# An MoE decode step: expert chunks of 32 rows instead of 64, their results summed in PSUM instead of gathered from DRAM

## What is computed

```python
def moe_ffn(h, w_router, b_router, w_up, b_up, w_down, b_down):
    xt = h.reshape(-1, D)                                   # 288 x 1024
    logits = (xt @ w_router + b_router).astype(jnp.float32)
    top_v, top_i = lax.top_k(logits, TOP_K)                 # 4 of 32
    wts = jax.nn.softmax(top_v, axis=-1)
    gate_dense = jnp.sum(jax.nn.one_hot(top_i, N_EXPERTS) * wts[..., None], axis=1)
    out = jnp.zeros_like(xt)
    for e in range(N_EXPERTS):
        z = xt @ w_up[e] + b_up[e]                          # 1024 -> 2048
        gate = jnp.minimum(z[:, :D_EXPERT], SWIGLU_LIMIT)
        up = jnp.clip(z[:, D_EXPERT:], -SWIGLU_LIMIT, SWIGLU_LIMIT)
        act = (up + 1.0) * gate * jax.nn.sigmoid(SWIGLU_ALPHA * gate)
        out = out + gate_dense[:, e:e + 1] * (act @ w_down[e] + b_down[e])   # 1024 -> 1024
    return out.reshape(B, T, D)
...
        y = y + g2 * rms_norm(moe_ffn(h, *moe_w), norm_ffn_post[l])
```

## Time and profile before

| | |
|---|---|
| median of 3 runs | 1501.06 us (1496.23 to 1505.27) |
| profiled execution | 1502.18 us |
| its span, first to last instruction | 1500.3 us |
| mean granted TensorE clock | 0.981 |
| TensorE matmul busy | 1391.5 us, 93% |
| VectorE, ScalarE, GpSimd busy | 372.8, 298.0, 80.3 us |
| moved by DMA | 513.31 MB, 342 GB/s over the span |
| chain that ended last | PE 70%, DMA 23%, VectorE 3% |

### The profile page before, as it was taken

How to read it: one execution, slowest core, us unless ns; L and a number is a source line. 1 busy time by engine, 2 the same in 40 slices (tenths; PEclk the granted TensorE clock), 3 DMA queues, 4 the chain that set the end, 5 groups by cost and what they waited for, 6 DMA issues and landing times.

```text
span 1500.3 us, 20784 instructions
## 1 busy us (share of the span) xinstructions
PE 1391.5 (93%) x8590; PEld 616.0 (41%) x8590; DVE 372.8 (25%) x858; ACT 298.0 (20%) x572; POOL 80.3 (5%) x107
## 2 busy tenths in 40 slices
PE   5999998799989999999999999999999998999894
PEld 4554555466766433333333333333333322333231
DVE  5220012377643531111121111211111111111125
ACT  5100005566421221101111111110111110111001
POOL 2000004000000000000000000000000000000000
PEclk9899999999999999999999999999999999999997
DMA  9985755124297899799999999999999999999995
GB/s 282 335 303 204 266 201 178 49 73 154 65 274 269 350 420 427 319 395 427 426 427 426 426 427 426 428 426 426 429 425 428 425 428 425 428 427 426 427 405 182
DMA packets 94787, 513.31 MB, mean 342 GB/s; under 512 B 12033, under 2 KB 41113, under 8 KB 67634
## 3 DMA queue, kind: packets, MB, share of 16 engines
q1 hardware_dynamic: 87986, 490.04, 81.8%
q0 software_dynamic: 6720, 22.06, 4.2%
HBM read 501.19 MB, written 19.22 MB: 347 GB/s over the span
## 4 chain that ended last, share of the span: by engine, by line
PE 70%; DMA 23%; DVE 3%; ACT 2%; issue 1%; SPq 1%; POOL 1%; POOLq 0%; DVEq 0%; ACTq 0%
PE bank L1460 21%; DMA arena<-in_w_up 18%; PE bank L1487 13%; PE bank L1417 5%; PE bank L818 4%; PE bank L1227 4%; PE bank L1058 3%; PE bank L1059 3%; DMA arena<-slots 2%; PE bank L1324 2%; DMA arena<-in_cache_cmp,arena 2%; PE bank L1450 1%; PE bank L1470 1%; PE bank L831 1%; PE bank L1423 1%
## 5 line engine op out<-in xcount | busy, mean ns | idle before, releaser
L1460 PE MATMUL bank<-arena 128*64 128x512 f32 x2176 | 481.5, 596 | 33.4 <-DMA arena<-in_w_up 33.4
L1460 PEld LDWEIGHTS bank<-arena 128*64 128x64 f32 x2176 | 150.6, 137 | 361.1 <-issue 300.4
L1487 PE MATMUL bank<-arena 128*64 128x512 f32 x1088 | 241.2, 595 | 0.4 <-DMA arena<-in_w_down 0.4
L2443 DVE TENSOR_SCALAR arena<-bank,arena 128x1 uint32<-128x1 f32 x33 | 7.2, 219 | 565.0 <-DMA slots<-arena 564.9
L1487 PEld LDWEIGHTS bank<-arena 128*64 128x64 f32 x1088 | 74.7, 136 | 141.1 <-issue 135.7
L1849 ACT ACTIVATE arena<-arena 128x512 f32<-128x512 f32 x34 | 21.4, 630 | 515.7 <-DVE arena L2447 515.7
L1417 PE MATMUL bank<-arena 128*64 128x512 f32 (+1 forms) x420 | 103.0, 607 | 0.0
L2543 POOL DMA_DIRECT2D slots<-arena x33 | 18.1, 547 | 1100.7 <-ACT arena L1859 1100.7
L1227 PE MATMUL bank<-arena 128*128 128x288 f32 x256 | 69.8, 420 | 2.9 <-DMA arena<-in_w_in 1.7
L2447 DVE TENSOR_SCALAR arena<-bank 128x512 f32<-128x512 f32 x34 | 23.5, 692 | 189.5 <-PE bank L1460 189.5
L1859 ACT COPY arena<-bank 128x512 f32<-128x512 f32 x33 | 19.3, 585 | 214.9 <-PE bank L1487 214.9
(11 more groups left out here) (455 smaller groups left out, 1242.0 us busy)
## 6 DMA issues: line engine op xcount, KB each, us to landing
arena<-in_w_up SPq DMA_DIRECT2D x128, 2048.0 KB, 33.3
arena<-in_w_down SPq DMA_DIRECT2D x64, 2048.0 KB, 33.0
arena<-in_w_ada SPq DMA_DIRECT2D x12, 2048.0 KB, 11.6
arena<-in_w_in SPq DMA_DIRECT2D x6, 2048.0 KB, 12.2
arena<-in_w_in SPq DMA_DIRECT2D x16, 512.0 KB, 4.3
arena<-in_state_win SPq DMA_DIRECT2D x4, 1024.0 KB, 10.6
arena<-in_w_out SPq DMA_DIRECT2D x1, 4096.0 KB, 17.4
arena<-slots SPq DMA_DIRECT2D x2, 2048.0 KB, 25.1
```

What stands on the lines that cost most here:

```text
L1460: last = mm(banks[part][SLOT * s:SLOT * s + SLOT, :], xcT[:, q], ring[n % R_][:, at:at + 512], start=False, stop=q == 7)
L1487: last = mm(banks[4][SLOT * s:SLOT * s + SLOT, :], lhs, ring[n % R_][:, at:at + 512], start=f == 0, stop=f == 7)
```

## The change

SLOT becomes 32. Of a chunk, 32 rows take a quarter of the output partitions, and four instructions with 32 columns of the array each stand side by side, each for another quarter of the weights' columns. `slots`, the indirect writes, `slot_rows` and the gather at the end are gone. Instead PSUM banks 3 to 7 hold the sums of all tokens through all experts: banks 4 to 7 the 256 prompt tokens, bank 3 the 32 sample tokens. After each chunk TensorE adds the chunk *before* to them: `owT` (the weights of that chunk's 32 rows by token, transposed) times `yc`. These products (L1462, L1468 of the new file) stand in the chunk behind the transposes of the activations and ahead of three transposes that make the next `owT` (L1456, L1457) and of the down products. The order of the transposes is turned: `chunk_T` first, then the activations'. The down biases are added once, ahead of expert 1. The rows of a `w_down` piece are laid out so that each partition gets two runs of 8 KB instead of one of 16 KB.

```diff
-SLOT = 64
+SLOT = 32
...
+            def up_products(c, e):
+                for q in range(8):
+                    n = 6 * e + q // 2
+                    if q % 2 == 0:
+                        pe.wait_ge(S(f"ld_piece{n % R_}"), 16 * (n // R_) + 16)
+                    for j in range(4):
+                        last = mm(banks[0][32 * j:32 * j + SLOT].rearrange("p (h c) -> p h c", h=2), xcT[:, q % 2, q // 2],
+                                  up_cols[n % R_][:, q % 2, j], start=q == 0, stop=q == 7)
+                    if q == 0:
+                        for r in range(4):
+                            mm(banks[0][32 * r:32 * r + SLOT, :], ident[32 * r:32 * r + E, 32 * r + e:32 * r + e + 1].broadcast_to([E, SLOT]),
+                               bias[32 * r:32 * r + E, :], start=False, stop=False)
+                    if q % 2:
+                        last.then_inc(S("up_used"), 1)
...
+            def add_prompt(i, shares, rows, r, start, stop):
+                for q in range(4):
+                    last = mm(banks[4 + q][:, 256 * i:256 * i + 256], shares[32 * q:32 * q + r, P * i:P * i + P],
+                              rows[32 * q:32 * q + r, 0:256], start=start, stop=stop)
+                return last
...
             for e in range(E):
                 before = pe.value_load(tab[0:1, E + e:E + e + 1], min_val=0, max_val=CMAX)
                 upto = pe.value_load(tab[0:1, e:e + 1], min_val=1, max_val=CMAX)
+                if e == 1:
+                    pe.wait_ge(S("owT"), before + 1)
+                    down_biases()
                 with pe.Fori(before, upto) as c:
                     pe.wait_ge(S("xcT"), c + 1)
-                    if e > 0:
-                        slot_rows(e)
...
+                    pe.wait_ge(S("owT"), c + 1)
+                    up_products(c, e)
                     pe.wait_ge(S("oneslot"), c + 2)
+                    pe.wait_ge(S("yc"), c + 1)
                     dispatch()
-                    pe.wait_ge(S("act"), c + 1)
-                    for k in range(4):
-                        last = nc.tensor.transpose(banks[(3, 6)[k // 2]][:, P * (k % 2):P * (k % 2) + P], up_fours[:, k], ident)
...
                     pe.wait_ge(S("xr"), c + 2)
                     chunk_T()
-                    pe.wait_ge(S("yc"), c)
...
+                    pe.wait_ge(S("act"), c + 1)
+                    for v in range(2):
+                        last = nc.tensor.transpose(banks[1][:, P * v:P * v + P], act_pairs[:, v], ident)
+                    last.then_inc(S("aT_ps"), 1)
+                    for i in range(2):
+                        add_prompt(i, owT, yc, SLOT, False, False)
+                    add_sample(owT, yc, SLOT, False, False)
+                    pe.wait_ge(S("ow"), c + 1)
+                    weights_T()
+                    down_products(c, e)
...
+                if n == PIECES - 1:
+                    sp.wait_ge(S("up_used"), until * 4 + 3)
+                    sp.dma_start(gate_p, modd[0:1, 3 * D:4 * D].broadcast_to([P, D])).then_inc(S("ld_last"), 16)
...
+                if q < 4:
+                    sp.wait_ge(S("up_used"), until * 4 + (q + 1))
+                else:
+                    sp.wait_ge(S("down_used"), until * 2 + (q - 3))
                 load_piece(n)
...
-            with pool.Fori(0, last_chunk) as c:
-
-                pool.wait_ge(S("yc"), c + 1)
-
-                pool.dma_start(slots[bass.ds(NRES + c, 1), 0:1], eps_t[0:1]).then_inc(S("st_yc"), 16)
-                pool.indirect_dma_start(out=results, out_offset=bass.IndirectOffsetOnAxis(ap=rowu[:, 0:1], axis=0), in_=yc, in_offset=None,
-                                        bounds_check=2 * NRES - 1, oob_is_err=False).then_inc(S("st_yc"), 16)
```

More of the change, by code:

```diff
@@ new lines, in down_products @@
+            def down_products(c, e):
+                pe.wait_ge(S("aT"), c + 1)
+                for m in range(2):
+                    n = 6 * e + 4 + m
+                    pe.wait_ge(S(f"ld_piece{n % R_}"), 16 * (n // R_) + 16)
+                    for v in range(2):
+                        for h in range(2):
+                            for j in range(4):
+                                last = mm(banks[1][32 * j:32 * j + SLOT, 256:512], aT[:, v, 2 * m + h], down_cols[n % R_][:, h, v, j],
+                                          start=m + v + h == 0, stop=m + v + h == 3)
+                    last.then_inc(S("down_used"), 1)
@@ new lines, in add_sample, with down_biases @@
+            def add_sample(shares, rows, r, start, stop):
+                for q in range(4):
+                    last = mm(banks[3][32 * q:32 * q + NS, 0:256], shares[32 * q:32 * q + r, TP:TP + NS],
+                              rows[32 * q:32 * q + r, 0:256], start=start, stop=stop)
+                return last
+            def down_biases():
+                after(pe, "dense4")
+                for i in range(3):
+                    last = nc.tensor.transpose(banks[0][:, P * i:P * i + ROWS[i]], dense4[0:ROWS[i], i].rearrange("p q e -> p (q e)"),
+                                               ident[0:ROWS[i], 0:ROWS[i]])
+                last.then_inc(S("wT_ps"), 1)
+                pe.wait_ge(S("ld_bdown"), 64)
+                after(pe, "wT")
+                for i in range(2):
+                    add_prompt(i, wT, bdown, E, False, False)
+                add_sample(wT, bdown, E, False, False)
@@ L1499, in _ @@
-            summed_in = ((0, 1), (2, 3), (6, 7))
-            def biases(i):
-                for v in range(2):
-                    q = 32 * (2 * (i % 2) + v)
-                    mm(banks[summed_in[i][v]][0:ROWS[i], :], wT[q:q + E, P * i:P * i + ROWS[i]], bdown[q:q + E], start=True, stop=False)
-            def chunk_part(i):
-                r = ROWS[i]
-                for v in range(2):
-                    last = mm(banks[summed_in[i][v]][0:r, :], owT[SLOT * v:SLOT * v + SLOT, P * i:P * i + r], yc[SLOT * v:SLOT * v + SLOT],
-                              start=False, stop=i < 2)
-                return last
@@ L1513, in _ @@
-            after(pe, "wT")
-            pe.wait_ge(S("ld_bdown"), 64)
-            for i in range(3):
-                biases(i)
-            for i in range(2):
-                chunk_part(i).then_inc(S(f"sum{i}"), 1)
-            chunk_part(2)
-            pe.wait_ge(S("ld_gath2"), 64)
-            for v in range(2):
-                last = mm(banks[6 + v][0:NS, :], wdiag, gath_s[:, 512 * v:512 * v + 512], start=False, stop=True)
-            last.then_inc(S("comb_ps"), 1)
+                    pe.wait_ge(S("act"), c + 1)
@@ L1526, in _ @@
+            pe.wait_ge(S("owT"), upto + 1)
+            for i in range(2):
+                add_prompt(i, owT, yc, SLOT, False, i == 1)
+            add_sample(owT, yc, SLOT, False, True).then_inc(S("sums"), 1)
+            after(pe, "sample_ss")
+            for j in range(4):
+                last = mm(banks[2][32 * j:32 * j + NS, 0:1], C("stack32"), ss[:, 3:4], start=True, stop=True)
+            last.then_inc(S("sample_parts"), 1)
         @block.scalar
@@ new lines, in _ @@
+            with act.Fori(0, first) as c:
+                chunk_step(c)
+            after(act, "wT_ps")
+            nc.scalar.copy(wT, banks[0][:, 0:TP + NS]).then_inc(S("wT"), 1)
+            with act.Fori(first, total) as c:
+                chunk_step(c)
+            act.wait_ge(S("sums"), 1)
+            for half in range(2):
+                if half:
+                    act.wait_ge(S("half_gated"), 1)
+                for i in range(2):
+                    last = fn(squares[2 * half + i], prompt_sum(i, half), ACT.Square,
+                              accum_out=sq2[:, i, half:half + 1])
+                last.then_inc(S("half_squared"), 1)
@@ L1874, in _ @@
-            last.then_inc(S("sq2"), 1)
-            root(2, 8)
+            after(act, "sample_parts")
+            fn(rt_[:, 2:3], banks[2][:, 0:1], ACT.Sqrt, bias=eps_t, scale=1.0 / D).then_inc(S("rms"), 1)
         @block.vector
@@ L2471, in _ @@
[L2471 to L2480 removed]
+                dve.wait_ge(S("aT_ps"), c + 1)
```

357 lines of the change are left out of this document (140 added, 217 removed).

## The result

The changed kernel takes **1529.64 us** (median of 4 runs, 1526.59 to 1532.99), the kernel before on the same chip 1500.3 us (4 runs, 1496.23 to 1505.27). The ratio is 1.0195, with a 95% interval of 1.0154 to 1.0235. The forecast was 1527, in a range of 1492 to 1550. The profiled execution has a span of 1525.6 us, against 1500.3 before.

The account below looks back on a forecast made before the run. PE and DMA were both taken as full, to be priced per expert. 1500.3 - 11.4 - 11.0 + 54.6 + 1.5 + 1.5 + 4 - 13.4 = 1526.1 us span; +1.9 around it, median 1.1 lower: 1527, range 1492 to 1550.

Parts of the forecast that it names:

- T: PE's time for one chunk of 32 rows: 16.5 us, with bounds of 14.6 and 17.5.
- Stalls of 54.6: DMA waits for PE at experts with several chunks: 26.4 us in runs of two, 4.2 at expert 3, 24.0 at expert 13.
- The old stall, -11.4: DMA time lost at two-chunk expert 3 in the kernel before, taken off the sum: 11.4 us.
- Written results, -11.0: Result rows no longer written to DRAM (4.7 MB) free 11.0 us of DMA time.
- Gates ahead of the last piece, +1.5: The last gates (0.65 MB) are loaded ahead of the last weight piece: 1.5 us more.
- Rows of 8 KB, +1.5: Down pieces come in rows of 8 KB instead of 16 KB: between 0 and 3 us more, 1.5 taken.
- Clock, +4: PE's clock drops where it waits for pieces, on entering runs of two-chunk experts: 4 us more, bounds 0 and 7.
- Tail, -13.4: After the last piece, without the gather: 20.3 us at half clock against 33.7 before, 13.4 less.
- the first: Rival: DMA-bound all the way; with T at 14.8 or less two chunks fit into 29.7 us: 1485 us, chance 0.12.
- The second: Rival: terms cancel, T about 15.7 by cheaper changes of shape and no clock loss: 1503 us, chance 0.16.
- the fourth: Rival: waiting for activations replaces waiting for rows, 0.3 us more per chunk: 1533 us, counted in the forecast's chance of 0.64.
- The third: Rival: four side by side don't keep pace, or clock drops reach chunks; T 18 to 19.6, about 1605 us, chance 0.08.

Follow-up runs that it names:

- the chunks of 64 rows: Changed kernel with chunks of 64 rows again, 34 of them, keeping the new sums in PSUM: 1545.38 us, ratio 1.0292 to the kernel before.
- the stores' experiment: Kernel with one chunk of 32 per expert, plus 32 stores of 128 KB of results to unread DRAM: 1474.41 us, 8.9 more than without the stores.
- the kernel with 14.0: Changed kernel without the sums of all chunks' results but the last, and without the up products' bias: 1485.47 us, ratio 0.9869 to the kernel before.
- the last kernel: Changed kernel, same result: sums before the wait, sample rows last in dispatch, up bias and one register load per expert, last gates later: 1491.74 us, ratio 0.9931.

## Why the prediction was right, point by point

The time, the sign and the mechanism came out as forecast: 1529.6 for 1527, by DMA that waits for PE in runs of experts with two chunks. Inside the sum several terms were off and made each other good, which is luck.

- **T = 16.5**: 16.59 within an expert. The single terms are all within 0.2 of their rows: bias 1.0 for 1.05, dispatch with the wait 2.24 for 2.2, sums 1.08 and 0.56 for 1.0 and 0.55, down products 3.47 for 3.55. What was missing is the 0.4 between experts.
- **Stalls of 54.6**: 67 against a clean piece (expert 3: 5.5, experts 4 to 6: 13.2, expert 13: 26.7, experts 14 to 18: 21.9). For an expert of two chunks I had 33.0 - 29.7 = 3.3; it is 33.8 - 29.4 = 4.4. Of the 1.1, 0.3 is the price of a piece (4.95 for 4.90), 0.2 the chunks, 0.4 the change of expert. Experts 8, 9, 12 and those after 18 lost nothing, as said, but for a longer piece now and then.
- **The old stall, -11.4**: 12.8 in the same reckoning. That expert 3 shows what any expert with two chunks does was a wrong reading of the old trace: expert 13 lost 0.4 there (see the chunks of 64 rows above). **Written results, -11.0**: about -10, by the stores' experiment.
- **Gates ahead of the last piece, +1.5**: the last piece came 7.2 us after the one before it, 5.9 in the kernel before, so +1.3. **Rows of 8 KB, +1.5**: 0; the down pieces land every 4.9 us like the others.
- **Clock, +4**: next to nothing before the last piece in the profiled execution, and that was chance. In the first experts PE waits almost 3 us for each piece, and of two pieces with the same wait one is used at full clock (1.93; granted clock 1.00 from 592 to 596 us) and one at half (3.55; 0.53 from 597.3 to 600.9):

```profile
592.46 1.93 PE L1433 MATMUL psum<-arena 128*32 128x512 f32 x16 [2.97 <-DMA arena<-in_w_up]
597.35 3.55 PE L1433 MATMUL psum<-arena 128*32 128x512 f32 x16 [2.97 <-DMA arena<-in_w_up]
```

  That is in the first chunk of expert 3, where it could have counted. PE came 1.6 us later to the down products, but the last piece for them landed only at 607.2, so all but some 0.3 of it was waited for anyway; expert 12's first chunk has the same at 884. In the experiment with the chunks in another order, which has the same numbers of chunks up to this place, the half clock lasted longer. Window 600 to 610 us of the changed kernel and then of that one (the last three numbers are the granted clock, DMA share and GB/s):

```profile
600.00:610.00 10.00, 9.51 (x135) 4.56 (x127) 3.26 (x8) 1.54 (x4) 0.00 (x0) 0.97 1.02 430
...
600.00:610.00 10.00, 9.51 (x67) 3.43 (x59) 2.04 (x5) 1.16 (x3) 0.00 (x0) 0.50 1.03 432
```

  There PE ended the chunk at 613.98 instead of 609.29, the last piece having landed at 608.0, and expert 3 lost 9.7 us instead of 5.5. So 4 is what the clock can cost at one entry into a long expert; which executions pay it, no run here says.

  The Trainium skill (*TensorE: Matmul & The Clock Gate*, HAM oscillation) says that thin matmuls which wait for DMA lose the full clock at every tile. By that rule the term would have been 7. Here some pieces lose it and many don't, and where they do a wait for the next piece mostly takes up what it costs.
- **Tail, -13.4**: -15.9. Of the 3.3 us for half clock only 1.5 came.
- **Sum up to the last piece**: +39.2 forecast, +44.6 measured; tail and start gave 2.5 and 3.4 back. So the 1526.1 of span for the measured 1525.6 is better than its parts. (The upper end of the range, 1550, is given as 1527 + 21, which is 1548; the measured time is far from either.)

Of the rivals, the first (T at or under 14.8 ends the stalls of two-chunk experts) held as a rule, shown by the kernel with 14.0, with the limit nearer to 14.5; but T was not there. The second, that T comes to 15.7 by cheaper changes of shape, and the fourth did not happen: the activations were never waited for, L1515 has no idle time. The third fell to the 0.43 per four instructions, and the clock drops reached into a chunk only here and there.

## What to carry to other kernels

Where a ring of buffers lies between two engines that are both nearly full, price each unit of work (here an expert) on both, and ask how many units in a row are above the bound and how much the ring can carry. The sum of the work decides nothing there: the same 52 chunks took 1530 us in one order and 1501 in another. Then look for work in the loop that needs nothing late and put it in front of the wait, not behind it, and move out of the inner loop what belongs to the outer one.

## What the hardware showed that I had not expected

- The loads land every 4.90 us (2 MB, 428 GB/s) with hardly any scatter, but about every thirtieth piece takes 1.3 us more (in the kernel with one chunk per expert the pieces 32, 64, 95, 125, 157 and 187, counted from 0, took 6.1 to 6.5 us). In the mean that is 0.04 a piece, most of the difference between 4.95 and 4.90. What it is was not tried.
- TensorE's granted clock fell to 0.913 of full in the mean (0.969 in the changed kernel) when PE waited at every piece, and the kernel was the fastest of all.
- Where two register loads stand between two loops of PE, it stood idle for 0.4 us in the kernel with chunks of 32 rows and not at all in the kernel before, whose last 32 products take 7 us instead of 3.5; with one load instead of two about 0.15 was left (962.96 to 966.55 at a change of expert, 948.28 to 951.73 within one, in the last kernel's timeline). That the loads are the cause is inferred: no run changed them alone.
